# MLP up projection: units 1 to 7 as seven half-size block products each, in alternation with the down halves

## The reference, cut to what matters

```python
h2 = rms_norm(x, norm_mlp[layer])
x = x + jnp.square(jax.nn.relu(h2 @ w_ff1[layer])) @ w_ff2[layer]
```

## Time and profile before

| | us |
|---|---|
| time, median of 3 runs | 1691.41 (1690.8 to 1692.02) |
| the profiled execution, its own time | 1689.05 |
| its span | 1687.4 |
| PE busy | 1672.0 (99%) |
| PEld busy | 1217.1 (72%) |
| DVE busy | 896.4 (53%) |
| ACT busy | 618.6 (37%) |
| granted clock, mean | 0.999 |

### The profile page before, as it was taken

How to read it: one execution, slowest core, us unless ns; L and a number is a source line. 1 busy time by engine, 2 the same in 40 slices (tenths; PEclk the granted TensorE clock), 3 DMA queues, 4 the chain that set the end, 5 groups by cost and what they waited for, 6 DMA issues and landing times.

```text
span 1687.4 us, 23046 instructions
## 1 busy us (share of the span) xinstructions
PE 1672.0 (99%) x9378; PEld 1217.1 (72%) x9378; DVE 896.4 (53%) x1217; ACT 618.6 (37%) x744; POOL 112.8 (7%) x168
## 2 busy tenths in 40 slices
PE   9999999999999999999999999999999999999998
PEld 7888888865454535454588877788888888888886
DVE  6425438452343334324668755567675544773487
ACT  6334433321111101111366633344642245652565
POOL 4000000000000000000011012210000001100100
PEclk9999999999999999999999999999999999999999
DMA  7332222948999999999541332124352358756974
GB/s 274 100 99 75 75 75 101 354 189 342 429 428 428 428 429 429 428 429 428 204 153 53 100 100 75 51 76 132 107 188 100 107 181 195 157 149 221 200 157 128
DMA packets 90703, 353.29 MB, mean 209 GB/s; under 512 B 7856, under 2 KB 7872, under 8 KB 78208
## 3 DMA queue, kind: packets, MB, share of 16 engines
q1 hardware_dynamic: 78288, 325.95, 50.4%
q0 software_dynamic: 12336, 26.23, 7.8%
HBM read 345.87 MB, written 6.29 MB: 209 GB/s over the span
## 4 chain that ended last, share of the span: by engine, by line
PE 97%; DMA 1%; DVE 1%; ACT 0%; issue 0%; POOL 0%; DVEq 0%; POOLq 0%; ACTq 0%
PE bank L2764 51%; PE bank L3117 12%; PE bank L3522 9%; PE bank L3130 7%; PE bank L3025 4%; PE bank L3065 3%; PE bank L3297 2%; PE bank L2789 2%; PE bank L2810 1%; DMA ring<-in_w 1%; PE bank L3327 1%; PE bank L3350 1%; PE bank L3397 1%; PE bank L3222 1%; PE bank L3430 0%; PE bank L3436 0%
## 5 line engine op out<-in xcount | busy, mean ns | idle before, releaser
L2764 PE MATMUL bank<-act_hi,w_hi 128*128 128x512 f32 x992 | 390.0, 393 | 0.0
L2764 PE MATMUL bank<-act_hi,w_lo 128*128 128x512 f32 x992 | 386.2, 389 | 0.0
L2764 PE MATMUL bank<-act_lo,w_hi 128*128 128x512 f32 x992 | 386.2, 389 | 0.0
L1754 DVE TENSOR_TENSOR w_lo<-w_stage,w_hi 128x2048 fp32r<-128x2048 f32 x79 | 181.1, 2293 | 208.9 <-ACT w_hi L1044 208.8
L1044 ACT ACTIVATE w_hi<-w_stage 128x2048 fp32r<-128x2048 f32 x79 | 151.4, 1917 | 242.0 <-PE bank L2764 223.7
L3117 PE MATMUL bank<-ring,xgT 128*64 128x512 f32 x992 | 216.1, 592 | 1.8 <-ACT xgT L1266 1.4
L2764 PEld LDWEIGHTS bank<-act_hi,w_hi 128*128 128x128 f32 x992 | 186.2, 188 | 40.8 <-issue 2.9
L2764 PEld LDWEIGHTS bank<-act_hi,w_lo 128*128 128x128 f32 x992 | 186.2, 188 | 39.1
L2764 PEld LDWEIGHTS bank<-act_lo,w_hi 128*128 128x128 f32 x992 | 186.3, 188 | 37.7
L3117 PEld LDWEIGHTS bank<-ring,xgT 128*64 128x64 f32 x992 | 71.0, 137 | 143.0 <-issue 139.5
L3130 PE MATMUL bank<-ring,gatedT 128*64 128x512 f32 x512 | 113.4, 595 | 3.1 <-DMA ring<-in_w 2.3
(11 more groups left out here) (490 smaller groups left out, 2366.6 us busy)
## 6 DMA issues: line engine op xcount, KB each, us to landing
ring<-in_w SPq DMA_DIRECT2D x94, 2048.0 KB, 16.8
w_stage<-in_w_in SPq DMA_DIRECT2D x42, 1024.0 KB, 5.1
w_stage<-in_w_ff SPq DMA_DIRECT2D x24, 1024.0 KB, 5.6
b_sum<-in_w_ff POOLq DMA_DIRECT2D x12, 1024.0 KB, 12.7
w_stage<-in_w_out SPq DMA_DIRECT2D x8, 1024.0 KB, 5.0
b_one<-in_w_ff SPq DMA_DIRECT2D x6, 1024.0 KB, 7.7
branch_gates<-gate_out POOLq DMA_DIRECT2D x16, 256.0 KB, 2.5
w_stage<-in_w_proj_gla SPq DMA_DIRECT2D x4, 1024.0 KB, 9.9
```

The source lines that it names most:

```text
L1754: dve.tensor_tensor(w_lo[s][:, 0:ktiles, :], w_stage[s][:, 0:ktiles, :], w_hi[s][:, 0:ktiles, :].bitcast(F32), ALU.subtract).then_inc(w_lo ...
L2764: ins = pe.matmul(banks[j][:, :], left, right, start=(kc == 0 and k == 0 and n_pass == 0), stop=(kc == g.chunks - 1 and k == g.ktiles - 1 ...
```

## The change

Unit 0 stays as it was, except that ACT squares its tiles too. Units 1 to 7 are each computed as seven block products of half size: the contraction is cut in two (512 rows each), the tokens in two (256 each) and the unit's columns in two (256 each). That gives, for each unit, 7 products of 2 x 4 x 3 = 24 matmuls of 128x256. The operands on the token side (`t_sum`, `t_hi`, `t_lo`, from a raw fp32 copy `raw_T` that ACT makes of the transposed rows) are made once, behind unit 0, three of them split anew in the second half. The operands on the weight side are made for each unit: four sums W1 to W4 on DVE (`w_add`), seven `hi` copies on ACT (`slot_high`) and seven `lo` subtractions on DVE (`slot_low`), all 128x1024, in three slots. Three partial results are copied out of PSUM by ACT (`copy_first`, `copy_both`, `copy_fifth`), three sums are formed by DVE (`blk_add`), and ACT does four relus and four squares of 128x512. The weight blocks of a unit (two of 1 MB) go through three buffers. The down halves keep their products; their two first activation parts and first weight steps are made among the work of the last unit of each half. SP's queue is written out anew.

The core of the diff, with the waits and the orders that the prediction speaks of:

```diff
-    g_ff = []
-    last = g_out2
-    for _ in range(HALVES):
-        up = Gemm(last, FH // 512, 2, "act")
-        last = Gemm(up, 2, PARTS, "dve", tiles=PARTS)
-        g_ff.append((up, last))
+    g_up = Gemm(g_out2, 1, 2, "act")
+    HALF_UNITS = FH // 512
+    BLOCKED = HALVES * HALF_UNITS - 1
+    g_blk, g_down, sums_added = [], [], []
+    for h in range(HALVES):
+        g_blk.append(Gemm(g_down[-1] if h else g_up, HALF_UNITS if h else HALF_UNITS - 1, PARTS, "act", tiles=3))
+        sums_added.append(g_blk[h].out["dve"])
+        g_blk[h].out["dve"] += 3 * g_blk[h].units
+        g_down.append(Gemm(g_blk[h], 2, PARTS, "dve", tiles=PARTS))
...
+        slot_page = (45, 41, 37)
+        slot_hi = [at(f"slot_hi{s}", page, [P, 4, 256], F32R) for s, page in enumerate(slot_page)]
+        slot_lo = [at(f"slot_lo{s}", page + 2, [P, 4, 256], F32R) for s, page in enumerate(slot_page)]
...
+        STAGE_ORDER = {0: [(1, 0), (2, 1), "v0", "v2", (5, 0), (6, 1), "v0", "v2"],
+                       1: [(1, 1), (3, 0), "v1", "v3", (4, 0), (5, 1), (7, 0), "v1", "v3"],
+                       2: [(2, 0), (3, 1), (4, 1), (6, 0), (7, 1)]}
...
+            def third_made(u):
+                sp.wait_ge(hid_summed, w_summed(u, W3))
+            def unit_split(u):
+                sp.wait_ge(w_lo_done, blk_split(u, 6))
...
+            sp.wait_ge(n_sd, rows_count(5, NT - 1))
+            load_sums(0)
+            sp.wait_ge(n_lo, T_LOWS + 3)
+            load_blocks(2, 0)
+            third_made(1)
+            load_blocks(2, 1)
+            unit_split(1)
+            load_blocks(3, 0)
+            load_ones(0)
+            third_made(2)
+            load_blocks(3, 1)
+            unit_split(2)
+            load_step(0, 0)
+            third_made(3)
+            load_step(0, 1)
+            for kc in range(2):
+                sp.wait_ge(w_lo_done, step(0, kc))
+                load_step(0, 2 + kc)
+            sp.wait_ge(part_low, V_PARTS + 3)
+            sp.wait_ge(hid_summed, summed_in(0) + S4)
+            sp.dma_start(b_one[0][:, :, :], weight_block(0, 1, 1, 0)).then_inc(b_one_in[0], 16)
+            sp.wait_ge(w_lo_done, step(0, 7))
+            load_blocks(4, 0)
+            load_blocks(5, 0)
+            sp.wait_ge(w_lo_done, step(0, 8))
+            sp.dma_start(b_one[1][:, :, :], weight_block(0, 1, 1, 1)).then_inc(b_one_in[1], 16)
+            sp.wait_ge(pe_tiles, 4 * (g_down[0].chunk0 + 12))
+            load_blocks(4, 1)
+            sp.wait_ge(w_lo_done, step(0, 13))
+            load_sums(1)
...
+                act.activation(raw_T[:, 4 * b:4 * b + 4, t * P:(t + 1) * P], turned, ACT.Copy).then_inc(raw_copied, 1)
...
+                act.wait_ge(pe_tiles, 4 * (before + max(m - 2, -1)))
...
+            t_high(T2)
+            t_high(T3)
+            for t in range(2):
+                mlp_squares(t)
+            slot_high(1, 0)
+            slot_high(1, 1)
+            for j in range(4):
+                act.wait_ge(pe_tiles, (g_up.chunk0 + 1) * 4 + j + 1)
+                if j >= 2:
+                    act.wait_ge(hid_sq, j - 1)
+                act.activation(relu_t[j % 2][:, :], gb[j][:, :], ACT.Relu).then_inc(out_act, 1)
+                act.wait_ge(out_act, g_up.tile0 + 4 + j + 1)
+                act.activation(hidden[:, j, :], relu_t[j % 2][:, :], ACT.Square).then_inc(hid_sq, 1)
+                if j in (1, 2):
+                    mlp_squares(j + 1)
...
+            def up_units(h):
+                units = units_of(h)
+                for u in units:
+                    first, last = u == units[0], u == units[-1]
+                    if first and h:
+                        t_high(T2, h)
+                    slot_high(u, 2)
+                    if first:
+                        t_high(T3 if h else T1, h)
+                    copy_first(u)
+                    slot_high(u, 3)
+                    if not first:
+                        relu_sum(u - 1, ADD_12, blk_both)
+                    slot_high(u, 4)
+                    if first:
+                        t_high(T4, h)
                     else:
+                        square(u - 1, 0, 1, blk_both)
+                        relu_last(u - 1)
+                    copy_both(u)
+                    if not first:
+                        square(u - 1, 1, 0, blk_last)
+                    slot_high(u, 5)
+                    copy_fifth(u)
+                    slot_high(u, 6)
+                    relu_sum(u, ADD_11, blk_first)
+                    if last:
+                        part_split_hi(h, 0)
+                    else:
+                        slot_high(u + 1, 0)
+                    square(u, 0, 0, blk_first)
+                    if last:
                         step_split_hi(h, 0)
-                    if u == 2:
-                        part_split_hi(h, 0)
-                    relu_unit(h, u)
-                    if u + 1 < up.units:
-                        split_hi(up.chunk0 + 2 * u + 3, 1)
-                    if u == 1:
-                        for kc in range(2):
-                            act.wait_ge(b_sum_in[kc], loaded(h, "sum", 1))
-                            negate(b_sum[kc], b_sum[kc])
-                    elif u == 2:
+                    else:
+                        slot_high(u + 1, 1)
+                    relu_sum(u, ADD_22, blk_fifth)
+                    square(u, 1, 1, blk_fifth)
+                    if u in (1, 4):
+                        negate_sums(0)
+                        negate_sums(1)
+                    elif u in (3, 6):
                         for kc, block in enumerate((b_one[1], b_far)):
                             act.wait_ge(b_one_in[1 - kc], loaded(h, "one", 1))
                             negate(block, block)
                 step_split_hi(h, 1)
+                relu_sum(units[-1], ADD_12, blk_both)
+                square(units[-1], 0, 1, blk_both)
+                relu_last(units[-1])
+                square(units[-1], 1, 0, blk_last)
                 part_split_hi(h, 1)
...
+            split_lo(g_up.chunk0 + 1, 1)
+            dve.wait_ge(raw_copied, NH + 2 * NT)
+            for n in (T1, T2, T3, T4):
+                t_add(n)
+            t_low(T2, 1)
+            t_low(T3, 2)
+            slot_low(1, 0)
+            slot_low(1, 1)
+            def up_units(h):
+                units = units_of(h)
+                for u in units:
+                    opening, closing = u == units[0], u == units[-1]
+                    first, second, third = blk_banks(u)
+                    w_add(u, W1)
+                    w_add(u, W2)
+                    if opening and h:
+                        for j in range(2):
+                            add_part(h - 1, 6, j)
+                        t_low(T2, 5)
+                    slot_low(u, 2)
+                    if opening:
+                        t_low(*((T3, 6) if h else (T1, 3)))
+                    slot_low(u, 3)
+                    w_add(u, W3)
+                    w_add(u, W4)
+                    slot_low(u, 4)
+                    if opening:
+                        t_low(T4, 7 if h else 4)
+                    if closing:
+                        sum_three(h)
+                    blk_add(u, ADD_11, 1, CP_FIRST, blk_first, second)
+                    slot_low(u, 5)
+                    slot_low(u, 6)
+                    if closing:
+                        part_split_lo(h, 0)
+                    blk_add(u, ADD_22, 4, CP_FIFTH, blk_fifth, first)
+                    if closing:
+                        step_split_lo(h, 0)
                     else:
-                        step_split_lo(h, 0)
-                    if u == 2:
-                        part_split_lo(h, 0)
-                        sum_three(h)
-                    hidden_unit(h, u)
-                    if u + 1 < up.units:
-                        split_lo(up.chunk0 + 2 * u + 3, 1)
+                        slot_low(u + 1, 0)
+                    blk_add(u, ADD_12, 5, CP_BOTH, blk_both, third)
+                    if not closing:
+                        slot_low(u + 1, 1)
                 step_split_lo(h, 1)
                 part_split_lo(h, 1)
...
+                elif n == 1 and u > 2:
+                    pe.wait_ge(out_dve, blk_added(u - 2, ADD_11))
+                elif n == 2:
+                    pe.wait_ge(out_act, blk_copied(u, CP_FIRST))
+                    pe.wait_ge(n_lo, T_LOWS + (5 if half_of_unit(u) else 1))
+                elif n == 3:
+                    pe.wait_ge(n_lo, T_LOWS + 3)
+                    if u > 2:
+                        pe.wait_ge(out_dve, blk_added(u - 2, ADD_12))
+                elif n == 4:
+                    pe.wait_ge(out_act, blk_copied(u, CP_BOTH))
+                    pe.wait_ge(n_lo, T_LOWS + (6 if half_of_unit(u) else 3))
+                elif n == 5:
+                    pe.wait_ge(out_act, blk_copied(u, CP_FIFTH))
+                elif n == 6:
+                    pe.wait_ge(n_lo, T_LOWS + (7 if half_of_unit(u) else 4))
```

(67 more changed lines are left out.)

332 lines of the change are left out of this document (222 added, 110 removed).

## The result

The changed kernel takes 1699.5 us (median of 5 executions, 1695.4 to 1700.9) against 1691.2 for the one before on the same chip: a ratio of 1.0050 (95% interval 1.0039 to 1.0061), **8.3 us slower**. The sign is that of the forecast's term sum (+3.1), the size is not. Nearly all of the 1.8 is the clock. Both kernels wait for a load at 815.5, 2.26 us before and 2.00 after; behind it before ran at full clock and the changed kernel fell to half, and matmul for matmul the lag grows there from 0.2 to 1.9 us.

A forecast was written before the change was run, and what follows sets the result against it. PE was taken to bound the kernel (97% of the chain): matmul count times distance, plus new waits. Stalls of 14.4 us against 11.3 saved gave +3.1, so 1691.4 became 1694.5 us; the range ran from 0.6 below 1686.8 up to 1700.

The forecast's parts named there:

- matmuls saved: Units 1 to 7: each takes 20.2 us instead of 21.8 at 0.120 us per 128x256 matmul, 11.3 us saved.
- item 1: Unit 1: raw copies and other work queued ahead delay product 2, and product 4 waits 0.2; 1.3 us stall.
- item 2: Closings of units 3 and 7: product 5 0.3 late in one, product 6 late behind the part split; 3.7 us.
- item 3: Down steps 1 and 2: waits of 0.7 and 1.4 in half 0, 0.2 in half 1; 2.3 us.
- item 4: Units 3 and 6: far-block loads share engines with accumulating DMAs, land in 12.6 us, product 2 is 1.5 late; 3.0 us.
- item 5: Step 3 of half 0: its load meets accumulating pair 3 and lands 12.1 us after issue; 4.1 us stall.
- load of step 11 behind those of units 4 and 5: SP's queue: due 1507, landing about 1503, split just in time; costed at nothing, 1 to 2.5 us if late.
- clock behind a wait: After a stall: a clock below full, never shown by the earlier windows, was left out of the sum.
- rival B: ACT and DVE: every half-size split costs more than its row; 1698.3 us, or 1700.8 at 0.1 more; chance 0.15.
- Rival A: Far-block and step 3 loads land in 5.4 to 6.4 us, uncaught by accumulations; 4.6 saved, 1686.8 us; chance 0.20.
- Rivals C and D: PE's matmul distance: C faster at 109 ns, 1691.3 us, chance 0.05; D slower at 0.1235, 1695.6 us, chance 0.05.
- the likeliest case: Forecast as laid out, landings of 11 to 13 us, 0.03 us on each instruction; 1691.5 to 1697.5 us; chance 0.50.

The follow-up runs named there:

- thin_adds: The changed kernel with each accumulating DMA of the MLP moving 64 of 512 columns (wrong weight sums, for timing only): 1686.4 us, ratio 0.9974.
- sum_first: The changed kernel with the addition for product 6 put ahead of the split of part 0 in units 3 and 7: 1697.5 us, ratio 1.0037.
- neg_late: The changed kernel with half 0's two negations of b_one moved behind the split of down step 2: 1696.7 us, ratio 1.0035.
- sums_apart: The changed kernel with the second contraction half of b_sum negated one unit later, in units 2 and 5: 1694.4 us, ratio 1.0022.
- one_first: The changed kernel with half 0's step 11 load ahead of the block loads of units 4 and 5 on SP's queue: 1699.0 us, ratio 1.0050.
- four: The changed kernel with the edits of neg_late, sum_first, one_first and sums_apart together: 1686.3 us, ratio 0.9965.
- again: The changed kernel once more, not edited: 1698.95 us, ratio 1.0048.
- sums_apart's second look: The kernel of sums_apart unedited, for one more profiled execution: 1694.2 us.
- one_first's second look: The kernel of one_first unedited, for one more profiled execution: 1697.0 us.

## Why the prediction was right and wrong, point by point

| step of the prediction | forecast | after |
|---|---|---|
| matmuls saved | -11.3 | 0.120 confirmed: 264 in 32.10, 192 in 23.05, and 648 in 77.92 of thin_adds |
| item 1, opening of unit 1 | 1.3 | 0.97 + 0.22 = 1.2 |
| item 2, closings of units 3 and 7 | 3.7 | 0.29 + 1.55 + 1.56 = 3.4 |
| item 3, down steps 1 and 2 | 2.3 | 0.56 + 1.27, half 1 0.25: 2.1 |
| item 4, far blocks of units 3 and 6 | 3.0 | 0.28 + 1.83 + 0.76 + 1.82 = 4.7 |
| item 5, step 3 of half 0 | 4.1 | 3.98 |
| load of step 11 behind those of units 4 and 5 | 0 | 1.7 |
| clock behind a wait | left out | 2.5 |
| smaller pieces | none | 1.5, of it 1.3 second starts |
| sum | +3.1 | +9.8 in the profiled MLP; +8.3 by the medians |

**What held.** Place, releaser and size of items 1, 2, 3 and 5 are within 0.3 us of the trace (for the wait at step 2 the trace names no releaser), and the experiments name the causes that the prediction gave: the part split ahead of a 0.69 us addition (sum_first), the negations ahead of step 1's split and pair 3 beside step 3's load (neg_late), the accumulating pair beside the far block (sums_apart, thin_adds). Far-block loads took 12.8 and 13.3 us for a forecast of 12.6, step 3's 12.1 for 12.1. The half-size instructions cost what the earlier trace rows gave: `slot_hi` 1053 ns, `slot_lo` 1223, the additions 683 to 689. So rival B is out, and middle units don't stall, as said. Rival A is out at full accumulation (its condition was a landing of 5.4 to 6.4), and thin_adds, which makes that condition true, gave 1686.4 where A had 1686.8. Rivals C and D are out by the distance. The Trainium skill, TensorE: Matmul & The Clock Gate (Back-to-back issue gap), would have given the estimate of 109 ns; thin_adds' 648 matmuls without a gap have 120.

**What failed: the sum, by 5.2 us of the medians.** Not one wrong mechanism, but four terms that were zero or short:

- *The clock, 2.5.* It was named as something that the sum left out, on the ground that no window of before shows it. But before has no wait in the MLP at all, against the 4.1 us that item 5 itself put there, so those windows could say nothing on it; and its wait of 2.26 at 815.5, ahead of the MLP, happened to be followed by full clock in that one execution. A forecast that adds a long wait to a stretch in which PE never waited had to carry this as a range.
- *Step 11, 1.7.* The edit was costed at nothing, "if late, 1 to 2.5 us", and it was late. The load landed at 1510.2, 14.6 us behind its issue at 1495.6, because the two block loads ahead of it on SP's queue shared the engines with an accumulation (landing 14.4); in one_first, where it goes ahead of them, it landed in 5.5 and step 11 doesn't wait. The rate of item 4, half of 262 GB/s, stood in the same text and wasn't applied to these three loads. Against the forecast PE came 5.9 us later to step 11 (1512.9 for 1507) and the load landed 7.2 later (1510.2 for 1503), and with no margin the difference of 1.3 is a wait.
- *Item 4, 1.7 short.* Slot 1 of unit 3 "still comes in time" was right within 0.3; in unit 6 it was not: product 1 was 0.76 late and product 2 1.82 instead of 1.5.
- *The small pieces, 1.5.* By the other ends of the table of kernels, time less waits less 287.8, they are 1.1 in thin_adds, 2.7 in the changed kernel (0.7 of it at the lower clock) and 3.1 in four. Most of it has a place. Behind each restart the second matmul starts 0.06 to 0.11 late too (behind 1384.94 it starts at 1385.13, 0.19 for 0.120), 15 times in the changed kernel, 1.3 in all; the restart's price was put at 0.15 and is nearer 0.25. Of the 3.1 in four, 1.5 is the lower clock in unit 7. All 1128 + 672 matmuls stand in the traces, so no missing record plays a part.

The forecast's sign was right and the time fell in the range, while the likeliest case's own range (up to 1697.5) missed it: it let landings and instruction times vary and held the number of waits fixed. That the whole range held it is in part luck: its upper end of 1700 was put there for rival B, slower splits, which the trace rules out.

## What to carry to other kernels

When plain loads and accumulating DMAs share the engines, move the issue of the accumulation before judging a scheme by its matmul count: here one scheme was 0.50% slower or 0.35% faster by where a few negations, one addition and one load stood in their queues. A load costed as "just in time" should be costed again with every DMA that its own queue and the others have under way at its issue, and a wait that is new to a stretch without waits can carry a second price, its clock: here 1.5 to 2.6 us each time, in some executions and not in others. It also falls in work that a change doesn't touch, so compare two executions stage by stage before giving a microsecond to the change. When single edits gain 0 to 5 us, try them together before dropping any: a wait removed alone is often met again a few steps later.

## What the runs showed of the hardware

Behind some of its waits TensorE was granted the lower clock for 3 to 5 us of full work. At step 3 of the changed kernel and of sum_first it fell while the engine still waited, elsewhere within 1.5 us of its restart. The length of the wait alone doesn't decide it:

| execution | wait of PE, us | granted clock behind it |
|---|---|---|
| the changed kernel, step 3 | 3.82 | half |
| again, step 3 | 3.65 | half |
| sum_first, step 3 | 3.64 | half |
| sums_apart, step 3 | 3.58 | full |
| its second look, step 3 | 3.33 | half |
| one_first's second look, step 3 | 3.19 | half |
| one_first, step 3 | 2.88 | full |
| before, at 815.5, ahead of the MLP | 2.26 | full |
| the changed kernel, at 815.7 | 2.00 | half |
| neg_late, step 11 | 1.98 | half |
| four, product 2 of unit 7 | 1.87 | half |
| sums_apart's second look, product 2 of unit 7 | 1.77 | full |
| sums_apart, product 2 of unit 7 | 1.73 | half |
| the changed kernel, step 11 | 1.52 | full |
| neg_late, at 384.0, far ahead of the MLP | 0.88 | half |

By the windows and starts behind them the cost was 1.5 to 2.6 us each time. What decides between full and half is left open: the same code had both. The wait of 2.0 to 2.3 us near 815, which every kernel here has, was followed by half clock in eight of the twelve traces and by full clock in four (before, neg_late, sum_first and sums_apart's second look); those of 1.66 to 1.68 at product 2 of units 3 and 6 were always followed by full clock.

An accumulating DMA of 1 MB doubled and more the landing of a plain load of the same size: the loads at step 3 and step 11 took 5.0, 5.1 and 5.5 us where hardly any data of an accumulation moved beside them or where it moved an eighth; those on which PE waited took 12.1 to 13.3 beside one, and 14.6 as the third load in a row. In one_first the load of step 11 was issued 0.26 us behind the accumulation and still landed in 5.5.
